# Three 256-column products of a weight tile in half a PSUM bank each, in place of a 512-column and a 256-column product over a whole bank

## The reference, cut to what matters

```python
h = h + mix
h = h + squared_relu_mlp(rms_norm(h, norm_mlp_g[i]), w_mlp_up[i], w_mlp_down[i])   # 2048 -> 8192 -> 2048
gate = jax.nn.sigmoid(rms_norm(h, norm_ple_g[i]) @ w_ple_gate[i])                  # 2048 -> 2048
h = h + (p[i] @ w_ple_proj[i]) * gate                                              # 256 -> 2048
```

## Time and profile before

| | us |
|---|---|
| median of 3 runs | 2427.11 |
| lowest, highest | 2415.29, 2431.84 |
| profiled execution, first to last instruction | 2426.7 |
| PE busy | 2377.3 (98%) |
| PEld busy | 2064.3 (85%) |
| DVE busy | 1601.0 (66%) |
| ACT busy | 1276.6 (53%) |

### The profile page before, as it was taken

One profiled execution on the slowest core, in us unless ns is written; L12 is line 12 of the kernel. 1 busy time (PEld: TensorE's weight loads), 2 busy tenths in 40 slices (PEclk: granted clock), 3 DMA queues, 4 the chain that ended last, 5 costly groups with the idle time before them and its releaser, 6 DMA issues.

```text
span 2426.7 us, 39317 instructions
## 1 busy us (share of the span) xinstructions
PE 2377.3 (98%) x13454; PEld 2064.3 (85%) x13454; DVE 1601.0 (66%) x1892; ACT 1276.6 (53%) x1632; POOL 2.1 (0%) x15
## 2 busy tenths in 40 slices
PE   7999999999999999999999999999999999999997
PEld 6878888888888888888888888888888888888886
DVE  8789986655555555667776766765556556556665
ACT  6665565444444444555565665555445444445553
POOL 0000000000000000000000000000000000000000
PEclk9999999999999999999999999999999999999998
DMA  7644456556565556555655554656565565565543
GB/s 233 204 130 137 133 163 193 188 183 188 183 188 184 185 186 186 182 189 169 194 180 168 167 156 146 197 180 194 185 186 188 185 185 187 184 187 182 188 159 104
DMA packets 432146, 431.03 MB, mean 178 GB/s; under 512 B 13136, under 2 KB 430032, under 8 KB 432080
## 3 DMA queue, kind: packets, MB, share of 16 engines
q1 hardware_dynamic: 432080, 430.20, 56.8%
HBM read 428.05 MB, written 2.10 MB: 177 GB/s over the span
## 4 chain that ended last, share of the span: by engine, by line
PE 92%; DVE 4%; ACT 2%; DMA 1%; issue 1%; DVEq 0%; SPq 0%; ACTq 0%
PE ps L399 56%; PE ps L400 28%; PE ps L396 2%; PE O L572 2%; PE ps L397 1%; DVE spl L1033 1%; ACT spl L632 0%; DMA raw<-in_w_o 0%; PE O L501 0%; DVE tv L1069 0%; PE Z L475 0%; DMA raw<-in_w_in 0%; PE ps L457 0%; DVE nacc L1097 0%; DVE h L1113 0%
## 5 line engine op out<-in xcount | busy, mean ns | idle before, releaser
L1033 DVE TENSOR_TENSOR spl<-raw,spl 128x1024 fp32r<-128x1024 f32 x810 | 980.1, 1223 | 543.3 <-ACT spl L632 517.5
L632 ACT ACTIVATE spl<-raw 128x1024 fp32r<-128x1024 f32 x810 | 842.4, 1054 | 708.8 <-PE ps L400 664.3
L399 PE MATMUL ps<-XA,spl 128*128 128x512 f32 x3072 | 1090.0, 400 | 15.4 <-DVE spl L1033 10.8
L399 PE MATMUL ps<-XB,spl 128*128 128x512 f32 x3072 | 1088.5, 399 | 0.5 <-DVE pp L1069 0.5
L400 PE MATMUL ps<-XA,spl 128*128 128x256 f32 x3072 | 863.4, 281 | 0.0
L400 PE MATMUL ps<-XB,spl 128*128 128x256 f32 x3072 | 862.4, 281 | 0.0
L399 PEld LDWEIGHTS ps<-XA,spl 128*128 128x128 f32 x3072 | 578.4, 188 | 158.8 <-issue 12.3
L399 PEld LDWEIGHTS ps<-XB,spl 128*128 128x128 f32 x3072 | 577.2, 188 | 143.5 <-issue 1.3
L400 PEld LDWEIGHTS ps<-XA,spl 128*128 128x128 f32 x3072 | 581.8, 189 | 0.4
L400 PEld LDWEIGHTS ps<-XB,spl 128*128 128x128 f32 x3072 | 580.4, 189 | 0.2
L1069 DVE TENSOR_TENSOR tv<-cross,ps 128x512 f32<-128x512 f32 x208 | 141.5, 680 | 41.0 <-ACT cross L632 40.8
(11 more groups left out here) (145 smaller groups left out, 892.6 us busy)
## 6 DMA issues: line engine op xcount, KB each, us to landing
raw<-in_w_up SPq DMA_DIRECT2D x256, 512.0 KB, 3.9
raw<-in_w_down SPq DMA_DIRECT2D x256, 512.0 KB, 3.5
raw<-in_w_qkv SPq DMA_DIRECT2D x96, 512.0 KB, 4.5
raw<-in_w_in SPq DMA_DIRECT2D x64, 512.0 KB, 4.4
raw<-in_w_gate SPq DMA_DIRECT2D x64, 512.0 KB, 4.2
raw<-in_w_out SPq DMA_DIRECT2D x32, 512.0 KB, 3.4
raw<-in_w_o SPq DMA_DIRECT2D x32, 512.0 KB, 4.6
raw<-in_w_proj SPq DMA_DIRECT2D x8, 512.0 KB, 4.3
```

The source lines that it names most:

```text
L399: pe.matmul(ps[:, b + o, :], w[:, q, 0, c], x[:, kt, :, :], start=start, stop=False)
L632: return act.activation(out, in_, ACT.Copy, scale=scale)
L1033: dve.tensor_tensor(s[:, :, 1, :], raw[:, m % NRAW, :, :], s[:, :, 0, :].bitcast(F32), ALU.subtract).then_inc(lo_ready, 1)
```

## The change

- `ps` becomes 4 banks of two 256-column halves. A whole group lives in one bank, half `o` for column half `o`; four groups rotate (`NACC = 4`), and TensorE waits for the reading of group `g-4` (`acc_taken`).
- `three` issues three 256-column matmuls in place of the pair. All three add to the same half bank.
- `cross`, `take_cross`, `take_sum` and `sum_ready` go. The first DVE instruction that used `tv` now reads the bank itself (`acc(g)`).
- In `ple`, ACT copies the bank to `pp`; DVE has no part in it.
- `nacc` becomes 512 wide: `fold` is one 512-wide add, `stats` two products in place of one.
- In `up`, ACT writes `hid` and `tv` by two squares, with no wait between them.
- DVE waits for the end of the group's last chunk itself, and its split of the fourth chunk ahead comes after the read of the bank.
- TensorE's loops in the MLP turn over four groups in place of two; other loops on TensorE, ACT and DVE are written out.

```diff
-        cross = sb("cross", [P, 2, T])
-        nacc = sb("nacc", [P, T])
+        nacc = sb("nacc", [P, 2, T])
-        ps = ctx.enter_context(nc.psum_tensor("ps", [P, 4, 512], F32))
+        ps = ctx.enter_context(nc.psum_tensor("ps", [P, NACC, 2, 256], F32))
...
+            def three(out, a, b, start, stop):
+                pe.matmul(out, a[0], b[0], start=start, stop=False, skip_group_check=True)
+                pe.matmul(out, a[0], b[1], start=False, stop=False, skip_group_check=True)
+                return pe.matmul(out, a[1], b[0], start=False, stop=stop, skip_group_check=True)
...
-                            pe.matmul(ps[:, b + o, :], w[:, q, 0, c], x[:, kt, :, :], start=start, stop=False)
-                            mm = pe.matmul(ps[:, b + o, 0:256], w[:, q, 1, c], x[:, kt, 0, :], start=False, stop=stop)
+                        mm = three(ps[:, g % NACC, o, :], a, b, first and q == 0 and o == 0, last and q == 3)
...
-                if counts(g - 1, gi):
-                    pe.wait_ge(sum_ready, gi + (g - 1))
+                if counts(gi + (g - 3)):
+                    pe.wait_ge(acc_taken, gi + (g - 3))
...
-                mm = pe.matmul(Z[:, 0, 0:256], onesD[:, :], nacc[:, :], start=True, stop=True)
+                for j in range(2):
+                    mm = pe.matmul(Z[:, 0, 0:256], onesD[:, :], nacc[:, j, :], start=(j == 0), stop=(j == 1),
+                                   skip_group_check=True)
...
-                with pe.Fori(0, 4) as i:
-                    for s in range(2):
-                        gemm(g + 8 + s, i * 2, m + 32 + 4 * s, i, hid,
+                with pe.Fori(0, 2) as i:
+                    for s in range(4):
+                        gemm(g + 8 + s, i * 4, m + 32 + 4 * s, i * 2, hid,
...
-            def take_cross(g, gi, ready):
-                ...
-                copy(cross[:, :, :], ps[:, b:b + 2, 256:512]).then_inc(cross_copied, 1)
...
+                    copy(pp[:, 2 * u:2 * u + 2, :], ps[:, (g + u) % NACC, :, :]).then_inc(acc_taken, 1)
...
-            def take_sum(g, gi, out=None):
-                ...
-                dve.tensor_tensor(tv[:, :, :] if out is None else out, cross[:, :, :], ps[:, b:b + 2, 0:256],
-                                  ALU.add).then_inc(sum_ready, 1)
+            def scaled(g, out):
+                dve.tensor_tensor(out, acc(g), bcast(rB[:, :], 2), ALU.mult).then_inc(acc_taken, 1)
...
-                dve.tensor_tensor(tv[:, 0, :], tv[:, 0, :], tv[:, 1, :], ALU.add).then_inc(sq_folded, 1)
-                dve.wait_ge(sq_folded, f * 2 + 1)
-                dve.tensor_tensor(nacc[:, :], nacc[:, :], tv[:, 0, :], ALU.add).then_inc(sq_folded, 1)
+                dve.tensor_tensor(nacc[:, :, :], nacc[:, :, :], tv[:, :, :], ALU.add).then_inc(sq_folded, 1)
```

More of the change, by code:

```diff
@@ L40 @@
 NSPL = 8
+NACC = 4
 EPS = 1e-6
@@ L228, in trunk, with counts @@
         lam_chain = sem("lam_chain")
-        def counts(base, turns):
-            return base > 0 or not isinstance(turns, int)
+        def counts(value):
+            return not isinstance(value, int) or value > 0
         def bcast(ap, n):
@@ L617, in _ @@
             pair(1, 0, False)
-            with pe.Fori(1, 4) as i:
+            for i in range(1, 4):
                 pair(0, i, False)
@@ L705, in residual, with up, gate @@
                     r.then_inc(out_scaled, 1)
-            def up(g, gi, m, it, u, t0, hid, norm_n=None, first=False):
-                group(g, gi, m, it, first)
+            def up(s, m, it, g, gi, u, t0, hid, norm_n=None, first=False):
+                group(s, m, it, first)
                 if norm_n is not None:
                     norm(norm_n)
[L711 to L717, removed]
+                taken(g, gi)
+                act.activation(hid[:, bass.ds(t0, 2), 0, :], tv[:, :, :], ACT.Square).then_inc(up_sq, 1)
+                act.activation(tv[:, :, :], tv[:, :, :], ACT.Square).then_inc(up_hi, 1)
+            def gate(s, m, it, g, gi, k, t0, n, X, norm_n=None, first=False):
+                group(s, m, it, first, 1)
                 if norm_n is not None:
                     norm(norm_n)
-                if not first:
-                    split(m + 2 + NSPL, it)
-                act.wait_ge(gate_scaled, k + 1)
+                taken(g, gi)
                 act.activation(tv[:, :, :], tv[:, :, :], ACT.Sigmoid).then_inc(gate_sig, 1)
@@ L982, in qkv @@
                 if first and part < 2:
-                    group(g, 0, m, 0, True)
+                    group(part, m, 0, True)
                 else:
@@ L989, in qkv @@
                             steps[q](s - 1, i)
-                        split(m + NSPL + q, i * 3)
-                if not (first and part < 2):
-                    take_cross(g, i * 6, group_done(m, i * 3))
+                        split(m + NSPL + q)
                 if first and part == 0:
                     norm(3, columns=True)
-                act.wait_ge(qk_scaled, i * 6 + (3 * s + part + 1))
+                taken(g, 0)
                 out = vv[s][:, :, 0, :] if part == 2 else qk[s][:, part, :, 0, :]
@@ L1130, in up, with down, gate @@
                 dve.wait_ge(up_tiles, u + 1)
-            def down(g, gi, m, it, hidx, t0, first=False, later=0, steps={}):
-                group(g, gi, m, it, first, later, steps)
-                dve.wait_ge(sum_ready, gi + (g + 1))
-                add_h(hidx, t0)
-            def gate(g, gi, m, it, k, f, hidx, t0, n, X, norm_n=None, first=False):
-                group(g, gi, m, it, first, 2)
+            def down(g, gi, s, m, it, t0, first=False, steps={}):
+                group(s, m, it, first, steps)
+                add_h(g, gi, t0)
+                if not first:
+                    split(m + 3 + NSPL, it)
+            def gate(g, gi, s, m, it, k, f, t0, n, X, norm_n=None, first=False):
+                group(s, m, it, first)
                 if norm_n is not None:
@@ L1141, in gate @@
                     clear(n)
-                scaled(g, gi, tv[:, :, :], gate_scaled)
-                if not first:
-                    split(m + 2 + NSPL, it)
+                scaled(g, tv[:, :, :])
                 dve.wait_ge(gate_sig, k + 1)
@@ L1202, in _, with gates @@
+            def gates(g, m, k, f, norm_in, n, X):
+                for s in range(8):
+                    gate(g + s, 0, s % 2, m + 4 * s, 0, k + s, f + s, 2 * s, n, X,
+                         norm_in if s == 0 else None, s < 2)
             lam = params[:, LAMBDA:LAMBDA + 8]
```

457 lines of the change are left out of this document (200 added, 257 removed).

## The result

| | before | after |
|---|---|---|
| median, us | 2421.2 (2399.45 to 2431.84, 4 runs) | 2470.0 (2469.49 to 2471.6, 4 runs) |
| profiled span, us | 2426.7 | 2467.8 |

The ratio is 1.023, with a 95% interval of 1.017 to 1.029: slower by more than 1%, as forecast with 2467 us, but not clear of 2%. One more run of before, beside the first three, came in at 2399 us. That before spreads so widely, and after by only 2 us, is taken up behind experiment 3. A later run of before took 3904 us at a granted clock of 0.56; it is a slow one and counts in no comparison.

What follows compares the result with a forecast made beforehand. PE, busy 98% of the span, was taken as the bound. Span 2426.7 + 48 (triples) - 11 (hand-overs) + 3 (statistics) = 2467 us; range 2430 to 2485 us.

Steps and rivals of the forecast that it cites:

- three signs of being wrong: MLP spacing under 118 ns, gaps at the turns of the loops, or PE waiting for `acc_taken`.
- The third matmul, +48 us: PE, 6464 places: a triple takes 360 ns where a pair took 352.6, 48 us more.
- rival 1: Triples on PE cost what the short run shows, 355 ns: 2434 us in all; chance 0.2.
- rival 2: Only columns count on PE: 346.5 ns a triple, 2380 us in all; chance 0.08.
- Hand-overs, -11 us: PE's waits in `ple`, for `sum_ready` and at the end shrink as `cross` and the sum go: 11 us less.
- Statistics, +3 us: `stats`, run seven times: a second product adds 14 records, between 0 and 6.6 us, taken as 3.
- Code, 0 in the sum: TensorE's longer loop bodies: by the skill's room for 2,048 instructions still held, so no cost and 2467 us.
- rival 3: Each of 18 MLP jumps back waits up to 3.9 us for code: 70 us more, 2537; chance 0.07.
- Moved steps, 0: DVE's wait and later split, SP's loads, ACT's splits and second square: covered by slack of 20 us, no cost.
- The ends of the range: Whole kernel: triples of 359 to 361 ns with 0 to 20 us saved, given as 2452 to 2480 us; chance 0.65.

Runs made afterwards that it cites:

- experiment 3: The kernel after with the pair of before (512 and 256 columns, two banks a group, two groups in rotation), bank's left half read directly: 2418.8 us, ratio 1.0031.
- Experiment 1: The kernel before with only its 512-column matmul issued as two of 256 columns in `chunk`: 2472.6 us, ratio to before 1.0268.
- experiment 5: The kernel before with each chunk's eight 512-column matmuls first, then its eight of 256 columns: 2408.9 us, ratio 0.9965.
- experiment 2: The kernel after with TensorE's outer MLP loop written out, inner loops over four groups kept: 2455.6 us.
- experiments 6 and 7: Kernel after, outer MLP loop written out; 6: second and third products 192 columns wide, 2342.7 us; 7: third product on 64 of 128 weight columns, 2393.5 us.
- experiment 8: The kernel before with order wide, wide, narrow, narrow, and the new hand-over only in `ple`: 2394.6 us, ratio to before 0.9909.

## Why the prediction was right, and where its terms were off

The time was 1 us from the span and 3 from the median. The main term and its reason were right. That the sum came so close was luck: the hand-overs brought 10 to 13 us more than forecast, and the stops on code, which the sum had at nothing, took 14.4. One of the three signs of being wrong came true, gaps at the turns of the loops; another came only in small, waits of 1.0 and 0.4 us for a bank in `ple`, less than the 2 us kept there.

- **The third matmul, +48 us: right.** Spacing 120 ns, 360 a triple. The trace before had the whole price in 18 matmuls of another stage, and of its two rows the longer run was the one to take. Experiment 1 paid it alone, 45 us between the two spans where 47 were expected; rival 1 with 355 ns and rival 2 with 346.5 are both out, and experiment 5 shows that a run of eight is already long enough.
- **Hand-overs, -11 us: mis-sized.** They brought 21 to 24. The sum gives 24 as what is left: 41.1 us of span, less 47.8 for the triples, 3.0 for the statistics and 14.4 for the stops; experiments 1 and 2 give 21, the 18 us between their spans and the 3 for the statistics. The terms that were priced came about as forecast: 7 us in `ple`, 3.2 for `sum_ready`, 1.7 at the end. Two things had been left out. `fold` was costed at nothing, but the first norm's chain of squares and folds is what PE waits for at 36 us, and that wait fell from 3.7 to 1.0 us. DVE's turn of one fold and one split there is 1.86 us in place of 2.05; from the first of the eight folds to the last that makes 1.5 us, and where the rest comes from stays open. And the stretches at half clock were not priced. Before has four of them; in experiment 2's kernel the same four places have none. First before, then that run, columns as above:

```profile
33.00:40.00 7.00, 3.96 (x15) 3.36 (x16) 6.31 (x9) 5.15 (x7) 0.00 (x0) 0.76 0.85 265
153.00:160.00 7.00, 6.19 (x22) 5.12 (x23) 6.88 (x15) 7.00 (x17) 0.00 (x0) 0.76 0.45 145
303.00:310.00 7.00, 4.54 (x17) 3.69 (x18) 6.63 (x7) 5.02 (x9) 0.00 (x0) 0.76 0.45 141
1488.00:1495.00 7.00, 5.17 (x20) 4.28 (x21) 4.08 (x6) 2.52 (x4) 0.00 (x0) 0.76 0.01 2
```
```profile
33.00:40.00 7.00, 6.13 (x49) 5.83 (x48) 5.52 (x6) 5.57 (x7) 0.00 (x0) 1.00 0.88 275
153.00:160.00 7.00, 6.74 (x52) 6.45 (x52) 7.00 (x14) 5.61 (x13) 0.00 (x0) 1.00 0.48 150
303.00:310.00 7.00, 5.55 (x45) 5.14 (x43) 4.21 (x4) 4.93 (x9) 0.00 (x0) 1.00 0.27 78
1505.00:1512.00 7.00, 7.00 (x59) 7.00 (x58) 3.57 (x4) 5.57 (x10) 0.00 (x0) 1.00 0.00 0
```

  A clock of 0.76 over 7 us is 3.4 us at 1.2 GHz in place of 2.4. At their start or just before it PE had stood idle for 3.5 to 4 us, at 1490 us in two parts of 1.3 and 2.8; with that idle time gone, or down to 1 to 2.3 us, the clock stays. Not each wait brings one: the two of 1.4 us, at 139 and 369 us, had none. Four times 3.4 us at half speed are at most 6.8 us, and idle time after the start fell by another 16.5 (26.9 to 10.4 without the stops).
- **Statistics, +3 us: right.** From the start of the last matmul before to that of the first after, four of the `stats` within the work take 0.79 us in place of 0.36, and a fifth 0.98 in place of 0.55; seven times 0.43 make 3.0.
- **Code, 0 in the sum: wrong, and rival 3 too dear.** The mechanism with 0.07 is there, at 2 jumps of 18 and 7.2 us each, 14.4 in all instead of 70. It had counted one landing, 3.9 us, for each jump; a stop is 4.8 us idle and a stretch at half clock. The Trainium skill's room for 2,048 instructions (Runtime: NRT & Kernel Launch, Instruction fetch mechanics) would have held the outer body of 1536; the trace has it fetched again in the first MLP and not in the second.
- **Moved steps, 0: right.** DVE's wait before the fourth split and ACT's copies in `ple` hold nothing up: the MLP has no gap but the two stops, and no wait of PE names them. The busy times came out a little over the forecast: DVE 1461 us for under 1460, ACT 1176 for under 1170. Neither is on PE's path.
- **The ends of the range.** The forecast's own terms give 2451 to 2484 us, not 2452 to 2480: 359 ns and 20 us saved, 361 ns and none saved.
- **Columns and loads.** The Trainium skill (TensorE: Matmul & The Clock Gate, Back-to-back issue gap) gives columns / 2.4 GHz plus 2.5 ns for a matmul by itself, and says that in a stream of loads and matmuls both set the spacing. The first would be 109 ns at 256 columns, an estimate from that page. The trace has 120 in all 425 us of experiment 1, and experiments 6 and 7 show the load in it, so it agrees with the second.

## What to carry to other kernels

Count loads, not only columns: in this kernel a 256-column matmul with its load takes 120 ns in a run, and joining two products with the same weights into one 512-column matmul saves 7 ns a place, 45 us in all, while the copy and the sum that it needs run on engines with time to spare. A cheaper hand-over is worth what PE waits for it, plus the half clock behind the longer of these waits; look for both in the waits and the clock before pricing it, and apply it only there (experiment 8). The price of a new instruction pattern may already stand in a corner of the trace; take the longest unbroken run of it.

## What had not been expected of the hardware

- The pair of 512 and 256 columns has two rhythms, 353 and 346 ns, and one program falls into either in different stages of one execution (experiment 3). Two long and two short ones in turn ran at 348 to 349 ns throughout, with runs within 5 us of each other.
- Jumps back over a loop body of 1536 matmuls and loads were free in one MLP and cost 7.2 us each in the other.
